# Transposes of x in four groups instead of three, the first two smaller, and meta rows loaded in two parts

## The chip, the cores and the metric

The kernel runs on one core of one Trainium2 chip. The metric is the device time of one execution in microseconds (us). The kernel before was timed in three runs.

## The reference, cut to what matters

One layer of a decoder trunk in float32. 16 meta tokens are put ahead of 256 tokens of x, which makes 272 tokens of 2048 features:

```python
h_res = concatenate([meta, x])                    # 272 x 2048
h = rmsnorm(h_res, pre_mix_g)
q_da, k_da, v_da, q_g, k_g, v_g, g_g, lr_g = split_cols(h @ w_in)   # 6144 + 16 columns
y = concatenate([diff_attention(...), gla(...)]) @ w_out            # 2048 x 2048
h_res = h_res + rmsnorm(y, post_mix_g)
y = conv_ffn(rmsnorm(h_res, pre_ffn_g), w_up, conv_w, conv_b, w_down)   # d_ff = 5632
out = (h_res + rmsnorm(y, post_ffn_g))[16:]
```

The change touches only the start: how x and the meta tokens reach the first columns of `h @ w_in`.

## The kernel before, in words

Every large product is done with split operands: a float32 matrix is written as hi + lo, both in a rounded format, and each product is hi·hi + hi·lo + lo·hi, three matmuls. Weights are streamed from memory by the queue of the sync engine SP in chunks of 128 x 1024 elements (512 KB) into eight buffers `raw`. A chunk has four blocks of 128 input features by 256 output columns. ScalarE (ACT) makes its hi part (`split_hi`, L358 to L362), then the lo part is made from both (`split_lo`, L364 to L367): by VectorE (DVE) for even chunks, by GpSimd (POOL) for odd ones (`lo_on_vector`, L50). TensorE (PE) then runs the chunk's 24 matmuls (`project_chunk`, L372 to L384), after waiting for the chunk's lo part. Four chunks make one pair of output tiles. Chunks 0 to 3 are the first pair; chunk c needs the input features 512·c to 512·c+511, that is tiles x_T 4c to 4c+3.

Those tiles come from x by transposes. SP loads x in four column blocks of 512 features (L451 to L454), each ahead of the weight chunk of the same number; the queue of ACT loads the first gain `pre_mix_g` (L555) and then the meta rows, 16 x 2048, in one transfer (L556). The step `x_T k` (L1335 to L1346) makes three transposes on PE into one of four side banks of PSUM: 16 meta rows and two blocks of 128 tokens. The step for k = 0 waits for the meta rows, each fourth for its block of x. ACT then writes `a_hi[k]`, scaled with the gain (L567). DVE writes a plain copy `xT[k]` (L864; for each fourth k ACT does it, L568) and `a_lo[k]` (L867), which frees the bank. For k < 8 a few matmuls without use follow (`busy`, L1317), five after k = 3 and one after each of the others.

All engines work their instructions in written order; nothing is planned at run time. `side_steps` (L55) says which small steps PE does after which chunk ("slot"). Before slot 0 stand the gain's transpose and x_T 0 to 7; after slot 0 x_T 8 to 11; after slot 1 x_T 12 to 15. On ACT the loop at L563 goes through the sixteen tiles and puts the first four hi splits among them:

```python
if k in (3, 5, 9, 11):
    split_hi(act_e, 0, (3, 5, 9, 11).index(k), first=True)
```

On DVE the loop at L859 does the lo split of chunk 0 after tile 3 and that of chunk 2 after tile 11; POOL does those of chunks 1 and 3 as soon as their hi parts are there (L508). PE waits before chunk c of the first pair for the release of its four tiles by DVE (L1530 to L1533). After the sixteen tiles ACT goes on with the hi split of chunk 4 and of later chunks, with the five squares of x (L577) between them.

Of the kernel before, what the change touches and what calls it, by code (L numbers as in the profile page):

```python
# [46 lines left out]
BANK = 512  # L47
# [7 lines left out]
def side_steps(slot, n_da, n_gla):  # L55


    steps = []
    if slot == -1:
        steps += [("pre_gain", 0)] + [("x_T", k) for k in range(8)]  # L60
    if slot in (0, 1):
        steps += [("x_T", k) for k in range(8 + 4 * slot, 12 + 4 * slot)]
    if slot == 5:
        steps += [("params", 0)]
    if slot == 6:
        steps += [("x_rms", 0)]
    if slot == 7:
        steps += [("lr", 0)]
    if slot == 8:
        steps += [("gates", hd) for hd in range(n_gla)]  # L70
    for h in range(n_da):
        for name, lag in (("scores", 0), ("probs_T", 3), ("attend", 5)):
            if slot == da_base(h) + lag:
                steps.append((name, h))
    for name, at in (("c_scores", C_BASE), ("c_T", C_BASE + 3), ("c_attend", C_BASE + 5)):
        if slot == at:
            steps.append((name, 0))
    if C_BASE + 8 <= slot < C_BASE + 8 + n_da:
        steps.append(("da_o_T", slot - C_BASE - 8))
    for hd in range(n_gla):  # L80
        for name, lag in (("v_T", 0), ("k_T", 3), ("kv", 5), ("gla_o", 7), ("gla_o_T", 10)):
            if slot == gla_base(hd) + lag:
                steps.append((name, hd))
    return steps
# [9 lines left out]
def da_base(h):  # L94


    return 12 * (h // 2 + 1) + 6 * (h % 2)


def gla_base(hd):  # L100
    return 60 + 8 * hd


def trunk(nc, x, meta_tokens, pre_mix_g, w_in, da_lambda, da_subln_g, gla_gate_w2, gla_gate_b, gla_norm_g,
          w_out, post_mix_g, pre_ffn_g, w_up, conv_w, conv_b, w_down, post_ffn_g, out):
    _, seq, d_model = x.shape
    n_meta = meta_tokens.shape[0]
    n_tok = n_meta + seq
# [55 lines left out]
    for slot in range(-1, IN1):  # L164
        for step in side_steps(slot, n_da, n_gla):
            first_turn[step] = turns
            turns += BANKS_OF[step[0]]
# [4 lines left out]
    with ExitStack() as ctx:  # L172
# [3 lines left out]
        def sem(name):  # L176
            return ctx.enter_context(nc.semaphore(name))
# [51 lines left out]
        def tile(t, n=1):  # L229
            return proj[:, t * n_tok:(t + n) * n_tok]  # L230
# [11 lines left out]
        def par_col(c):  # L242
            return par[:, c:c + 1]

        def tap(n, t):
# [4 lines left out]
        x_nat = tile(25, 23)[:, 0:3 * d_model].rearrange("p (t f) -> p t f", t=3)  # L250
# [51 lines left out]


        x_landed = [sem(f"x_landed{n}") for n in range(4)]
        meta_landed, gain_landed, par_landed, lam_landed, w2_landed, tail_landed, g_row_landed = (
            sem(n) for n in ("meta_landed", "gain_landed", "par_landed", "lam_landed", "w2_landed",
                             "tail_landed", "g_row_landed"))
        raw_landed = [sem(f"raw_landed{j}") for j in range(RAW)]
        hi_ready = sem("hi_ready")
# [48 lines left out]
        def split_hi(eng, rev, j, first=False):  # L358
            eng.wait_ge(raw_landed[j], rev * 16 + 16)
            if not first:  # L360
                eng.wait_ge(chunk_used, rev * RAW + (j - SPLIT + 1))
            eng.activation(w_hi[:, j % SPLIT, :], raw[:, j, :], ACT.Copy).then_inc(hi_ready, 1)  # L362
# [27 lines left out]
        def bank_of(step, n=0):  # L390
            return 4 + turn(step, n) % SIDE

        def await_free(pe, step, n=0):
            if turn(step, n) >= SIDE:
                pe.wait_ge(side_free[turn(step, n) % SIDE], turn(step, n) // SIDE)

        def await_full(eng, step, n=0):
            eng.wait_ge(side_full[turn(step, n) % SIDE], turn(step, n) // SIDE + 1)
# [5 lines left out]
        def full(step, n=0):  # L404
            return side_full[turn(step, n) % SIDE]
# [145 lines left out]
        def _(act_e):  # L551
            link = chain(act_e, act_chain)
            copy = lambda dst, src: act_e.activation(dst, src, ACT.Copy)

            act_e.dma_start(par_rows[0:KT, :], pre_mix_g[0].rearrange("(k p) -> k p", p=P)).then_inc(gain_landed, 16)  # L555
            act_e.dma_start(x_nat[0:n_meta, 2, :], meta_tokens).then_inc(meta_landed, 16)  # L556


            act_e.wait_ge(consts_made, 2)
# [3 lines left out]
            for k in range(KT):  # L563
                step = ("x_T", k)
                await_full(act_e, step)
                src = psum[:, bank_of(step), 0:n_tok]
                act_e.activation(a_hi[:, k, :], src, ACT.Copy, scale=par_col(G_PRE + k)).then_inc(x_hi_ready, 1)  # L567
                if k % 4 == 0:  # L568
                    copy(xT[:, k, :], src).then_inc(x_copied, 1)
                if k in (3, 5, 9, 11):  # L570
                    split_hi(act_e, 0, (3, 5, 9, 11).index(k), first=True)

            def x_square(n):

# [15 lines left out]
            for slot in range(IN1):  # L590
# [31 lines left out]
                for h in range(n_da):  # L622
# [9 lines left out]
                    if lag == 0:  # L632
# [7 lines left out]
                        for c in range(2):  # L640
                            for q, (_, _, a, b) in enumerate(DA_Q):
                                n = 2 * c + q
# [207 lines left out]
        def _(dve):  # L850
# [28 lines left out]
            for slot in range(IN1):  # L879
# [45 lines left out]
                if slot == 6 or slot % 4 == 3 and slot > 3:  # L925

                    p = slot // 4 if slot % 4 == 3 else 0
                    _, t0, kind = pairs[p]
                    a = Q0 if kind == "q" else 0
                    dve.wait_ge(chunk_used, 4 * p + 4)  # L930
                    for m in range(2):
                        dve.tensor_tensor(tile(t0 + m)[:, a:n_tok], psum[:, 2 * (p % 2) + m, 0:n_tok - a],  # L932
                                          rb[:, a:n_tok], ALU.mult).then_inc(tiles_evacuated, 1)
# [14 lines left out]
                for h in range(n_da):  # L948
                    lag = slot - da_base(h)
                    if lag == 0:  # L950

                        step = ("scores", h)
                        for c in range(2):
                            await_full(dve, step, 1 + c)
                            for q, (_, _, a, b) in enumerate(DA_Q):
                                n = 2 * c + q
                                ins = dve.tensor_reduce(s_max[:, n:n + 1], psum[:, bank_of(step, 1 + c), a:b], AX.X,
                                                        ALU.max)
                        link(ins)
                        dve.tensor_scalar(s_bias[:], s_max[:], -da_scale, None, ALU.mult).then_inc(bias_ready, 1)  # L960
# [343 lines left out]
        def _(pe):  # L1304
            def transposes(bank, sources):

                for col, src in sources:
                    rows, cols = src.shape
                    mm = pe.transpose(psum[0:cols, bank, col:col + rows], src, ident[0:rows, 0:rows])  # L1309
                return mm  # L1310
# [6 lines left out]
            def busy(bank, n):  # L1317

                for _ in range(n):
                    pe.matmul(psum[:, bank, 0:P], ones[:], ident[:], start=True, stop=True)  # L1320
# [14 lines left out]
            def x_T(step):  # L1335
                k = step[1]
                if k == 0:
                    pe.wait_ge(meta_landed, 16)
                if k % 4 == 0:
                    pe.wait_ge(x_landed[k // 4], 16)  # L1340
                await_free(pe, step)
                f = slice(k * P, (k + 1) * P)
                transposes(bank_of(step), [(0, x_nat[0:n_meta, 2, f]), (n_meta, x_nat[:, 0, f]),
                                           (n_meta + P, x_nat[:, 1, f])]).then_inc(full(step), 1)
                if k < 8:
                    busy(3, 5 if k == 3 else 1)  # L1346

            def x_rms(step):

# [162 lines left out]
            def gla_o_T(step):  # L1512
                hd = step[1]
                pe.wait_ge(og_scaled, 2 * hd + 2)
                for v in range(2):
# [3 lines left out]
                        .then_inc(full(step, v), 1)  # L1519

            emit = {"pre_gain": pre_gain, "params": params, "x_T": x_T, "x_rms": x_rms, "lr": lr, "gates": gates,
                    "scores": scores, "probs_T": probs_T, "attend": attend, "c_scores": c_scores, "c_T": c_T,
                    "c_attend": c_attend,
                    "da_o_T": da_o_T, "v_T": v_T, "k_T": k_T, "kv": kv, "gla_o": gla_o, "gla_o_T": gla_o_T}

            for step in side_steps(-1, n_da, n_gla):
                emit[step[0]](step)
            for slot in range(IN1):
                p, kind = slot // 4, pairs[slot // 4][2]
                if p == 0:  # L1530

                    for k in range(4 * slot, 4 * slot + 4):
                        await_evacuated(pe, ("x_T", k))  # L1533
                if slot % 4 == 0 and p >= 2:
                    pe.wait_ge(tiles_evacuated, 2 * (p - 1))
                project_chunk(pe, slot // RAW, slot % RAW, 2 * (p % 2), Q0 if kind == "q" else 0, n_tok)
                for step in side_steps(slot, n_da, n_gla):
                    emit[step[0]](step)
# [93 lines left out]
            for bank in range(8):  # L1632
                t, h, n = bank // 4, bank // 2 % 2, bank % 2
# [31 lines left out]
```

## Time and profile before

| what | value |
|---|---|
| median of 3 runs (lowest to highest) | 1294.6 us (1293.31 to 1294.68) |
| span of the profiled execution | 1294.8 us |
| PE busy | 1272.3 us, 98% |
| DVE, ACT, POOL busy | 664.1, 609.6, 505.7 us |
| memory traffic | 209.30 MB read, 163 GB/s over the span |

The profiled execution is given by its span alone; it lies 0.2 us above the median and 0.1 us above the slowest of the three runs. The page divides the span into 40 slices; the change lies in the first two of them, so windows of the trace are more use here than the page.

### The profile page before, as it was taken

The numbers are of one execution on the slowest core, as the hardware profiler recorded it, in microseconds if no ns is written. First come the engines' busy times: TensorE is split into PE (matmuls) and PEld (weight loads), VectorE is DVE, ScalarE is ACT, GpSimd is POOL, SyncE is SP. The second block draws the span as 40 slices with busy tenths as digits, with TensorE's granted clock in tenths as the row PEclk, the third lists the DMA queues.
The fourth block names the chain that finished last, engine by engine and source line by source line (L and its number), as shares of the span: only waits on it lengthen the run. The fifth ranks groups of instructions, "written<-read, shape, count | busy, mean of one in ns | idle before, by whom it ended". The sixth has DMA issues, their size and how long they took to land.

```text
span 1294.8 us, 24260 instructions
## 1 busy us (share of the span) xinstructions
PE 1272.3 (98%) x9194; PEld 1193.0 (92%) x9194; DVE 664.1 (51%) x963; ACT 609.6 (47%) x928; POOL 505.7 (39%) x231
## 2 busy tenths in 40 slices
PE   8989999999999999899999999999999999999997
PEld 7989999998888999899999999999999988888885
DVE  5353433447455534876666666666666652222224
ACT  5543443444555544554444545445454454444444
POOL 2232232232233443433444444444444444444443
PEclk8989999999999999899999999999999999999999
DMA  9534444443344556255565555656556555555551
GB/s 267 160 98 133 129 137 135 120 148 114 116 133 151 184 174 201 85 161 178 169 188 182 183 179 170 193 179 181 178 175 194 178 195 190 186 187 185 191 178 65
DMA packets 178105, 212.08 MB, mean 164 GB/s; under 512 B 8659, under 2 KB 164842, under 8 KB 177914
## 3 DMA queue, kind: packets, MB, share of 16 engines
q1 hardware_dynamic: 177850, 210.24, 52.2%
q10 hardware_dynamic: 208, 1.19, 0.3%
q8 instruction: 33, 0.54, 0.2%
q14 instruction: 14, 0.11, 0.0%
HBM read 209.30 MB, written 2.10 MB: 163 GB/s over the span
## 4 chain that ended last, share of the span: by engine, by line
PE 93%; DVE 5%; ACT 1%; DMA 1%; issue 0%; DVEq 0%; ACTq 0%
PE psum L382 66%; PE psum L1611 18%; PE psum L1309 2%; PE psum L1393 1%; DVE a_lo L1146 1%; DVE a_lo L876 1%; PE psum L1420 1%; DVE temp L946 1%; PE psum L1488 1%; PE psum L1395 1%; DMA proj<-in_meta_tokens 1%; PE psum L1421 1%; DVE w_lo L366 1%; PE psum L1639 0%; PE psum L1365 0%
## 5 line engine op out<-in xcount | busy, mean ns | idle before, releaser
L366 POOL TENSOR_TENSOR w_lo<-raw,w_hi 128x1024 fp32r<-128x1024 f32 x196 | 485.9, 2479 | 760.9 <-ACT w_hi L362 760.9
L382 PE MATMUL psum<-a_hi,w_hi 128*128 128x258 f32 (+1 forms) x2432 | 700.7, 288 | 3.5 <-DVE w_lo L366 1.4
L382 PE MATMUL psum<-a_hi,w_lo 128*128 128x258 f32 (+1 forms) x2432 | 697.6, 287 | 0.0
L382 PE MATMUL psum<-a_lo,w_hi 128*128 128x258 f32 (+1 forms) x2432 | 694.7, 286 | 0.0
L362 ACT ACTIVATE w_hi<-raw 128x1024 fp32r<-128x1024 f32 x392 | 412.4, 1059 | 526.2 <-PE psum L382 396.8
L366 DVE TENSOR_TENSOR w_lo<-raw,w_hi 128x1024 fp32r<-128x1024 f32 x196 | 261.6, 1335 | 447.5 <-ACT w_hi L362 446.5
L382 PEld LDWEIGHTS psum<-a_hi,w_hi 128*128 128x128 f32 x2432 | 465.2, 191 | 10.8 <-issue 7.0
L382 PEld LDWEIGHTS psum<-a_hi,w_lo 128*128 128x128 f32 x2432 | 465.2, 191 | 0.0
L382 PEld LDWEIGHTS psum<-a_lo,w_hi 128*128 128x128 f32 x2432 | 464.1, 191 | 0.0
L1611 PE MATMUL psum<-w_hi,a_hi 128*128 128x512 f32 x336 | 132.1, 393 | 0.0
L1611 PE MATMUL psum<-w_lo,a_hi 128*128 128x512 f32 x336 | 132.0, 393 | 0.0
L1611 PE MATMUL psum<-w_hi,a_lo 128*128 128x512 f32 x336 | 131.8, 392 | 0.0
L1201 DVE SCALAR_TENSOR_TENSOR proj<-proj,par 128x256 f32<-128x256 f32 x88 | 111.4, 1265 | 38.5 <-ACT proj L772 38.5
L1611 PEld LDWEIGHTS psum<-w_lo,a_hi 128*128 128x128 f32 x336 | 63.1, 188 | 14.4
L1611 PEld LDWEIGHTS psum<-w_hi,a_lo 128*128 128x128 f32 x336 | 63.1, 188 | 14.3
L1611 PEld LDWEIGHTS psum<-w_hi,a_hi 128*128 128x128 f32 x336 | 63.2, 188 | 14.1
L1204 DVE SCALAR_TENSOR_TENSOR proj<-proj,par 128x256 f32<-128x256 f32 x88 | 42.7, 485 | 11.6 <-DVE proj L1201 2.6
L772 ACT ACTIVATE proj<-proj,par 128x256 f32<-128x256 f32 x88 | 47.6, 589 | 1.6 <-DVE proj L1195 1.5
L778 ACT ACTIVATE proj<-proj 128x256 f32<-128x256 f32 x44 | 18.4, 420 | 63.0 <-DVE proj L1204 63.0
L1195 DVE TENSOR_TENSOR proj<-psum,rb 128x258 f32<-128x258 f32 x88 | 33.4, 421 | 15.5 <-PE psum L382 13.5
L1309 PE MATMUL psum<-ident,proj 128*128 128x128 f32 (+5 forms) x130 | 22.9, 277 | 5.6 <-DVE proj L932 3.7
L932 DVE TENSOR_TENSOR proj<-psum,rb 128x272 f32<-128x272 f32 (+1 forms) x48 | 18.6, 428 | 17.6 <-PE psum L382 17.5
(230 smaller groups left out, 673.6 us busy)
## 6 DMA issues: line engine op xcount, KB each, us to landing
raw<-in_w_up SPq DMA_DIRECT2D x176, 512.0 KB, 3.6
raw<-in_w_in SPq DMA_DIRECT2D x96, 512.0 KB, 3.8
raw<-in_w_down SPq DMA_DIRECT2D x88, 512.0 KB, 3.6
raw<-in_w_out SPq DMA_DIRECT2D x32, 512.0 KB, 3.5
proj<-in_x SPq DMA_DIRECT2D x4, 512.0 KB, 9.3
temp<-in_post_ffn_g ACTq DMA_DIRECT2D x1, 1024.0 KB, 8.0
out<-proj SPq DMA_DIRECT2D x2, 512.0 KB, 2.6
out<-proj SPq DMA_DIRECT2D x4, 256.0 KB, 2.6
```

The costliest lines, as they stand in the source:

```text
L362: eng.activation(w_hi[:, j % SPLIT, :], raw[:, j, :], ACT.Copy).then_inc(hi_ready, 1)
L366: eng.tensor_tensor(w_lo[:, j % SPLIT, :], raw[:, j, :], w_hi[:, j % SPLIT, :], ALU.subtract)\
L382: mm = pe.matmul(psum[:, bank + m, 0:t1 - t0], w[:, j % SPLIT, cols], a[:, k, t0:t1], start=(k == 0 and step == 0), stop=(k == KT - 1 and ...
L772: act_e.activation(c_sb[:, t, :], u_sb[:, m, NM:NQ], ACT.Identity, scale=tap(2, i * 2 + (m + NF * half)), bias=tap(3, i * 2 + (m + NF * ha ...
L778: act_e.activation(c_sb[:, m, :], c_sb[:, m, :], ACT.Silu).then_inc(silu_done, 1)
L876: dve.tensor_tensor(a_lo[:, k, 0:NQ], heads_tile(k), a_hi[:, k, 0:NQ], ALU.subtract)\
L932: dve.tensor_tensor(tile(t0 + m)[:, a:n_tok], psum[:, 2 * (p % 2) + m, 0:n_tok - a], rb[:, a:n_tok], ALU.mult).then_inc(tiles_evacuated, 1)
L1195: dve.tensor_tensor(u_sb[:, m, :], psum[:, t, 0:NQ], rb2[:], ALU.mult).then_inc(tiles_evacuated, 1)
L1201: dve.scalar_tensor_tensor(out=c_sb[:, t, :], in0=u_sb[:, m, 1:1 + seq], scalar=tap(1, w), in1=c_sb[:, t, :], op0=ALU.mult, op1=ALU.add).t ...
L1204: dve.scalar_tensor_tensor(out=c_sb[:, t, :], in0=u_sb[:, m, 0:seq], scalar=tap(0, w), in1=c_sb[:, t, :], op0=ALU.mult, op1=ALU.add).then_ ...
L1309: mm = pe.transpose(psum[0:cols, bank, col:col + rows], src, ident[0:rows, 0:rows])
L1611: mm = pe.matmul(psum[:, bank, :], a[:, j // 2, t * P:(t + 1) * P], w[:, j % SPLIT, n * BANK:(n + 1) * BANK], start=(first and s == 0), st ...
```

## The change

The diff, whole but for the list of semaphores:

```diff
@@ side_steps @@
     if slot == -1:
-        steps += [("pre_gain", 0)] + [("x_T", k) for k in range(8)]
-    if slot in (0, 1):
-        steps += [("x_T", k) for k in range(8 + 4 * slot, 12 + 4 * slot)]
+        steps += [("pre_gain", 0)] + [("x_T", k) for k in range(4)]
+    if slot in (0, 1, 2):
+        steps += [("x_T", k) for k in range(4 + 4 * slot, 8 + 4 * slot)]
@@ ScalarE @@
+            act_e.dma_start(x_nat[0:n_meta, 2, 0:BANK], meta_tokens[:, 0:BANK]).then_inc(meta_landed, 16)
             act_e.dma_start(par_rows[0:KT, :], pre_mix_g[0].rearrange("(k p) -> k p", p=P)).then_inc(gain_landed, 16)
-            act_e.dma_start(x_nat[0:n_meta, 2, :], meta_tokens).then_inc(meta_landed, 16)
+            act_e.dma_start(x_nat[0:n_meta, 2, BANK:d_model], meta_tokens[:, BANK:d_model]).then_inc(meta_rest_landed, 16)
@@
-                if k in (3, 5, 9, 11):
-                    split_hi(act_e, 0, (3, 5, 9, 11).index(k), first=True)
+                if k % 4 == 3:
+                    split_hi(act_e, 0, k // 4, first=True)
@@ TensorE, x_T @@
                 if k == 0:
                     pe.wait_ge(meta_landed, 16)
+                if k == 4:
+                    pe.wait_ge(meta_rest_landed, 16)
                 if k % 4 == 0:
                     pe.wait_ge(x_landed[k // 4], 16)
...
-                if k < 8:
-                    busy(3, 5 if k == 3 else 1)
+                if k < 4:
+                    busy(3, 8 if k == 3 else 1)
```

PE now does x_T 0 to 3, chunk 0, x_T 4 to 7, chunk 1, x_T 8 to 11, chunk 2, x_T 12 to 15, chunk 3. ACT makes the hi part of chunk c after `a_hi` of tile 4c+3. The meta rows come as a block of 512 features ahead of the gain on ACT's queue and the other 1536 behind it. Eight useless matmuls follow x_T 3, one each x_T 0 to 2, none x_T 4 to 7. Everything else is as before.

## Rows read from the trace of the kernel before

**Rows 1.** The page: busy time of the engines, and the chain that ended last.

```profile
PE 1272.3 (98%) x9194; PEld 1193.0 (92%) x9194; DVE 664.1 (51%) x963; ACT 609.6 (47%) x928; POOL 505.7 (39%) x231
...
PE 93%; DVE 5%; ACT 1%; DMA 1%; issue 0%; DVEq 0%; ACTq 0%
```

**Rows 2.** Chain of waits from 0 to 80 us: start, us, what.

```profile
1.32 6.70 DMA proj<-in_meta_tokens
...
17.93 2.87 PE psum L382 x24
...
25.48 3.22 DVE w_lo L366
28.70 0.14 issue
28.84 13.50 PE psum L382 x96
...
56.03 3.02 PE psum L382 x24
```

**Rows 3.** DMA issues that touch 0 to 1 us, with time to landing.

```profile
proj<-in_x SPq DMA_DIRECT2D x1, 512.0 KB, 5.8
proj<-in_pre_mix_g ACTq DMA_DIRECT2D x1, 8.0 KB, 3.7
```

**Rows 4.** Timeline to chunk 0: start, us, engine, line, operation, [idle before <-releaser].

```profile
0.83 0.44 SPq L453 DMA_DIRECT2D proj<-in_x  x1
...
8.06 0.60 PE L1309 MATMUL psum<-ident,proj 16*128 16x16 f32 x3 [1.88 <-DMA proj<-in_meta_tokens]
...
13.82 1.23 DVE L366 TENSOR_TENSOR w_lo<-raw,w_hi 128x1024 fp32r<-128x1024 f32 x1
...
16.62 1.05 ACT L362 ACTIVATE w_hi<-raw 128x1024 fp32r<-128x1024 f32 x1
...
17.68 0.36 PE L382 MATMUL psum<-a_hi,w_hi 128*128 128x258 f32 x1
17.75 2.41 POOL L366 TENSOR_TENSOR w_lo<-raw,w_hi 128x1024 fp32r<-128x1024 f32 x1 [13.10 <-ACT w_hi L362]
```

**Rows 5.** Timeline, transposes x_T 8 to 11 and chunk 1.

```profile
20.73 2.19 PE L1309 MATMUL psum<-ident,proj 16*128 16x16 f32 x12
...
22.24 0.50 DVE L867 SCALAR_TENSOR_TENSOR a_lo<-psum,par,a_hi 128x272 fp32r<-128x272 f32 x1 [2.56 <-ACT xT L553]
...
22.68 0.36 PE L382 MATMUL psum<-a_hi,w_hi 128*128 128x258 f32 x1
```

**Rows 6.** Timeline, transposes x_T 12 to 15 and the work behind them.

```profile
25.40 3.29 DVE L366 TENSOR_TENSOR w_lo<-raw,w_hi 128x1024 fp32r<-128x1024 f32 x1
25.74 2.19 PE L1309 MATMUL psum<-ident,proj 16*128 16x16 f32 x12
...
28.35 1.05 ACT L362 ACTIVATE w_hi<-raw 128x1024 fp32r<-128x1024 f32 x1
29.02 0.43 DVE L864 COPY xT<-psum 128x272 f32<-128x272 f32 x1
...
29.78 0.43 DVE L864 COPY xT<-psum 128x272 f32<-128x272 f32 x1
```

**Rows 7.** Windows: stretch, length, busy PE, PEld, DVE, ACT, POOL, PEclk (1.00 full), DMA share, GB/s.

```profile
7.00:8.00 1.00, 0.00 (x0) 0.00 (x0) 0.00 (x0) 0.00 (x0) 0.00 (x0) 1.00 1.06 291
8.00:9.00 1.00, 0.94 (x6) 0.71 (x6) 0.00 (x0) 0.22 (x1) 0.00 (x0) 0.83 1.04 373
...
25.73:28.84 3.11, 2.20 (x14) 1.37 (x13) 3.11 (x2) 2.42 (x6) 1.88 (x1) 1.00 1.09 368
28.84:33.10 4.26, 4.26 (x23) 4.26 (x24) 3.67 (x8) 4.26 (x7) 0.60 (x1) 0.60 1.06 340
...
78.00:83.00 5.00, 5.00 (x20) 4.02 (x21) 0.82 (x3) 1.54 (x3) 0.00 (x0) 0.50 0.88 298
```

**Rows 8.** Waits of SP's queue, 0 to 80 us: who waited for whom, total, times, longest.

```profile
SPq L356 <- POOL w_lo L366: 24.6, 5, 8.6
```

More of the change, by code:

```diff
@@ L304, in trunk @@
         x_landed = [sem(f"x_landed{n}") for n in range(4)]
-        meta_landed, gain_landed, par_landed, lam_landed, w2_landed, tail_landed, g_row_landed = (
-            sem(n) for n in ("meta_landed", "gain_landed", "par_landed", "lam_landed", "w2_landed",
+        meta_landed, meta_rest_landed, gain_landed, par_landed, lam_landed, w2_landed, tail_landed, g_row_landed = (
+            sem(n) for n in ("meta_landed", "meta_rest_landed", "gain_landed", "par_landed", "lam_landed", "w2_landed",
                              "tail_landed", "g_row_landed"))
```

## The prediction

> **What bounds the kernel now.** I read the page first. PE is busy 98% of the span, and 93% of the chain that ended last runs over it [rows 1]. So the rest of the kernel has next to nothing that could swallow a delay of PE or hand one back; what counts is at which moment PE leaves the stretch that the change touches. The second view is the chain of waits over the first 80 us [rows 2]. It enters through the landing of the meta rows, runs over PE to the end of chunk 1, leaves PE once for DVE's lo split of chunk 2, and then stays on PE for 96 matmuls (chunks 2 to 5) from 28.84 to 42.34 us. A chunk later on takes 3.02 us, chunk 1 took 25.73 - 22.68 = 3.05. With the last two of the four at 3.02, chunk 3 ended at 42.34 - 6.04 = 36.3 us. That is my yardstick: what the change does to 36.3 it does to the end. SP's queue waits for the splits there, not the splits for SP [rows 8], so loads don't bound this stretch.
>
> **The third view, the timeline, gives the pace of one group of four tiles.** Call T the start of its first transpose on PE.
> PE: the twelve transposes take 2.19 us [rows 5, 6].
> ACT: in the last group, T = 25.74, the hi split behind the fourth `a_hi` runs from 28.35 to 29.40, so it begins at T+2.6 and ends at T+3.7 [rows 6].
> DVE: the first `a_lo` starts at 22.24, with T = 20.73, and takes 0.50, so it ends at T+2.0 [rows 5]. Each further tile takes 0.76 us, the step between two copies (29.02 and 29.78) [rows 6]. Four tiles are through at T+4.3.
> Lo split: on DVE it comes behind this and takes 1.23 us [rows 4], so it ends at T+5.5. On POOL it begins 0.08 us after the hi split and takes 2.41 [rows 4], which gives T+6.15, with PE's reaction T+6.2.
>
> **Part 1: the groups come one later, and their hi splits with them.** This is the costly part. Before, PE ran x_T 4 to 7 ahead of chunk 0, and the hi split of chunk 1 stood after tile 5; it was done at 17.67, and POOL's lo split ran under chunk 0 (17.75 to 20.16) [rows 4]. Likewise x_T 8 to 11 ran ahead of chunk 1 and served chunk 2. Each split chain thus had a whole chunk of 3 us of PE work over it, and still chunk 2 was late: PE finished its transposes at 27.93 and started at 28.84, when DVE's split ended [rows 2, 6]. That split took 3.29 us instead of 1.23 because POOL's split of chunk 3 ran beside it; I take it that this stall goes, since in the new order POOL has nothing to do while chunk 2 is split.
> Now PE ends chunk c, does the four transposes that chunk c+1 needs, and has nothing behind them: the next instruction in its queue is chunk c+1 itself. From T to its start:
> - chunk 1 (POOL): 6.2 us, of which 2.2 are transposes, 4.0 idle
> - chunk 2 (DVE): 5.5 us, 3.3 idle
> - chunk 3 (POOL): 6.2 us, 4.0 idle
>
> Together 17.9 us, 11.3 of them idle. Behind the waiting PE stands everything; ACT, DVE and POOL have no work that could be drawn forward, as their queues wait for the same tiles. Below this I see no cheaper bound than the hi split moved by a few tenths. Above, transposes at half clock would make each group about 1.4 longer (below).
>
> **Part 2: the start.** PE waited 1.88 us for the meta rows, until 8.05 [rows 4]; they landed at 1.32 + 6.70 = 8.02 [rows 2]. x block 0, issued at 0.83, landed 5.8 later, at 6.6 [rows 3, 4]. The first quarter of the meta rows is now issued first on ACT's queue. The trace has no transfer of its size: 8 KB took 3.7 us and the whole 128 KB 6.7. From 0.82 on that means a landing between 4.5 and 7.5; I take one before 6.6, so x block 0 releases the first transpose at 6.65, a gain of 1.4. The gain's transfer, now 0.5 us later, lands near 5.0 and its transpose is done before that. The other meta rows, issued about 1 us after the first, have until after chunk 0.
> From T = 6.65 the pace above gives lo split 0 on DVE done at 6.65 + 4.3 + 1.23 = 12.2 us, where chunk 0 starts, since PE's transposes and eight useless matmuls are through by about 10.5. If the clock is at half, as before in this place, the pace is that of before, 15.05 - 8.06 = 7.0 [rows 4], and the start is 13.65. Chunk 0 started at 17.68, because x_T 4 to 7 stood ahead of it. So the start gives 4.0 to 5.5 us. One useless matmul fewer is nothing beside this.
>
> **Part 3: the clock.** Before chunk 2 PE idled 0.9 us, and right after it the granted clock was at its lower level: 0.60 on average over 28.84 to 33.10, where 23 matmuls took the 4.26 us [rows 7]. Chunks 2 to 5 took 13.50 us against 4 x 3.04 = 12.16, so one fall cost 1.34 us. It also fell after the idle stretch before 8.05. The new order has four idle stretches, 1.7 us ahead of chunk 0 and three of 3.3 to 4.0. I charge each chunk one fall: 4 x 1.34 = 5.4. The lower end is 0, were the clock never to fall; the upper is below.
> The row shows the clock at full through x_T 12 to 15 and the idle time behind them (PEclk 1.00, PE busy 2.20 of 3.11 us), and down right after [rows 7]. The Trainium skill ("TensorE: Matmul & The Clock Gate", Part 4) says that transposes don't count as PE-busy in the way matmuls do. By that rule the useless matmuls left out behind x_T 4 to 7 are missed, and the clock may stay down through the groups too; that is rival B.
>
> **Sum.** 12.2 + 4 x 3.04 + 17.9 + 5.4 = 47.7 us for the end of chunk 3, against 36.3: +11.4.
>
> **What comes behind.** ACT has five squares to do between its next hi splits (now some 2 us later against chunk 3's end), but chunk 4's hi split stands ahead of them, and by the same durations each later chunk is split 1 us or more ahead of PE. I take nothing, with 0.5 us as the upper bound for the row of the rms. The weight stream has eight buffers and is released by the same splits, so it shifts with PE.
>
> The profiled execution has a span of 1294.8 us, 0.2 above the median of the runs. 1294.8 + 11.4 = 1306.2; brought to the median, 1306.0 us.
>
> **Rivals.**
> A. The chain is as forecast but the clock never falls: without the 5.4, +6.0, 1300.6 us. For it: single falls before followed on quiet stretches of different kinds. Against: 0.9 us of idle was already enough behind the same transposes. Chance 0.12.
> B. The clock stays down over the whole stretch. For it: from 78 to 83 us, after an idle stretch of 3.7 us, PE was busy throughout with 20 small operations and the clock stood at 0.50 [rows 7]. The price: one fall cost 1.34 us in about 3.4 us at the lower level (0.60 over 4.26), 0.39 per us. A chunk of 3.04 then takes 5.0, four of them +7.8, and the three groups of 2.2 take 3.6, +4.2, together 12.0 instead of 5.4: 1312.6 us. Against: chunks are dense, and the clock came back within chunk 2 before. Chance 0.08.
> C. The other side: the waits between the groups are hidden, so that PE runs 4 x 3.04 + 3 x 2.2 = 18.8 us from 12.2 on and ends chunk 3 at 31.0, 5.3 earlier: 1289.3 us. It is one mechanism, the time from the last transpose of a group to its chunk, and it decides at 5.3 / 3 = 1.8 us per group. It would need the split chain to start before its fourth tile. The rows say 3.3 to 4.0, and ACT's order in the diff puts the hi split behind tile 4c+3. Chance 0.04.
> D. The meta part doesn't land sooner than the whole did (three transfers share the engines from 1.3 us on): the first transpose stays at 8.05, chunk 0 starts at 15.05, +2.9 on the forecast: 1308.9 us. This is the case in which the change doesn't do what it says. Chance 0.12.
> The forecast itself has the rest, 0.64, with its own range from 1303 to 1309.5 (start 12.2 or 13.65, one fall more or less of 1.34, the 0.5 behind).
>
> **How the numbers follow.** A, the forecast, D and half of B lie between 1300 and 1311.5; that holds well over 8 in 10, and I pull the ends in no further, since A and B are the bounds of the one unknown price. What this kernel's measurement can tell from no change is 0.2%, 2.6 us. Slower by more: everything but C and a remainder of mixtures, 0.95. Within 0.2%: 0.02. Faster: 0.03.
>
> **What would show it.** In the profile after: the first transpose near 6.7 us with x as its releaser; chunk 0 at 12 to 14; PE idle 3 to 4 us ahead of each of chunks 1, 2 and 3, released by a lo split, POOL's, DVE's, POOL's; DVE's split of chunk 2 at 1.2 us instead of 3.29; the granted clock below 1.00 in each of the four chunks; chunk 3 ending near 48 us; and from there on the same distances as before. I am wrong if PE finds chunk 1 split within 1.8 us of its last transpose, or if a wait far behind takes up the delay.

## The result: 1.1% slower, and the profile after

The changed kernel takes 1307.3 us (median of 4 runs, 1306.04 to 1309.2) against 1294.0 (median of 4, 1293.31 to 1294.68): +13.3 us, ratio 1.011 with an interval from 1.0085 to 1.0136. Forecast were 1306.0 us and a range from 1300 to 1311.5. The profiled execution has a span of 1306.8 us, 12.0 more than [rows 1]'s.

The page after: busy time, and the chain that ended last. PE's busy time grew by 1.6 us, its idle time from 1294.8 - 1272.3 = 22.5 to 1306.8 - 1273.9 = 32.9 us: 10.4 of the 12.0 us are idle time.

```profile
PE 1273.9 (97%) x9192; PEld 1193.9 (91%) x9192; DVE 664.8 (51%) x963; ACT 609.0 (47%) x928; POOL 505.7 (39%) x231
...
PE 93%; DVE 5%; ACT 1%; issue 1%; DMA 0%; POOL 0%; DVEq 0%; ACTq 0%
```

The chain of waits after (start, us, what), to be read against [rows 2]. It enters through the gain and no longer through the meta rows, and leaves PE ahead of each of the four chunks, where before it left PE ahead of chunk 2 alone:

```profile
1.31 4.83 DMA proj<-in_pre_mix_g
...
8.48 0.83 PE psum L1310 x3
...
14.60 1.24 DVE w_lo L366
15.83 0.14 issue
15.96 3.12 PE psum L382 x24
19.08 2.14 PE psum L1310 x12
...
22.76 2.35 POOL w_lo L366
25.11 0.14 issue
25.25 4.46 PE psum L382 x24
...
33.92 1.14 DVE w_lo L366
35.06 0.14 issue
35.20 4.57 PE psum L382 x24
39.77 2.13 PE psum L1310 x12
...
43.44 2.37 POOL w_lo L366
45.80 0.14 issue
45.94 10.39 PE psum L382 x72
...
70.01 3.02 PE psum L382 x24
```

PE's waits over the whole execution after: who waited for whom, total, times, longest. Before, the waits for a lo split came to 1.4 us in two; now there are 8.1 for POOL's and 4.1 for DVE's. All later waits (3.7, 3.2 us and so on) are as before.

```profile
PE psum L382 <- POOL w_lo L366: 8.1, 2, 4.0
PE psum L382 <- DVE w_lo L366: 4.1, 3, 3.4
PE psum L1310 <- DVE proj L933: 3.7, 1, 3.7
```

Windows after over chunks 1, 2 and 3 (columns as in [rows 7]): each chunk runs partly at the lower clock, as chunk 2 did before.

```profile
25.25:29.71 4.46, 4.46 (x25) 4.32 (x25) 0.00 (x0) 0.00 (x0) 0.00 (x0) 0.66 1.10 346
35.20:39.77 4.57, 4.57 (x25) 4.44 (x25) 0.00 (x0) 0.00 (x0) 0.00 (x0) 0.64 0.38 115
45.94:50.27 4.33, 4.33 (x25) 4.33 (x26) 0.93 (x1) 4.33 (x9) 2.39 (x1) 0.68 0.76 238
```

Chunks 3 to 5 end at 45.94 + 10.39 = 56.33, so chunk 3 ended near 50.3, against 36.3 before: 14.0 us late. The last chunk of this stretch, at 56.03 before [rows 2], begins at 70.01: still 14.0. The span shows 12.0. Of the 2.0 between them, about 1.5 are one fall of the clock that the traced execution of before had and that of after had not. The rows are the window right behind the small matmuls of one attention head, first before, then after:

```profile
203.00:207.00 4.00, 4.00 (x21) 3.93 (x20) 0.83 (x3) 1.77 (x8) 0.00 (x0) 0.57 0.44 131
```

```profile
217.00:221.00 4.00, 4.00 (x34) 4.00 (x33) 1.56 (x6) 2.84 (x9) 0.00 (x0) 1.00 0.40 125
```

The 72 matmuls there took 10.73 us before and 9.24 after. The remaining 0.5 us was not traced further. So single executions of one kernel differ by where the clock falls; those of before in the comparisons below (17, 23 and 29 executions) ran from 1288.7 to 1296.5 us, with medians of 1293.4 to 1293.6. That is why the experiments are judged by medians and intervals first, and a profile only for what happened within it.

### The profile page after: what moved, and what is told of

It is laid out like the page before. It is cut to its first block, busy times and chain, and to the rows that moved or that the text cites. A ratio compares the mean times of both kernels' runs of the same rounds, so it can differ in the third digit from the quotient of the medians.

```text
span 1306.8 us, 24257 instructions
## 1 busy us (share of the span) xinstructions
PE 1273.9 (97%) x9192; PEld 1193.9 (91%) x9192; DVE 664.8 (51%) x963; ACT 609.0 (47%) x928; POOL 505.7 (39%) x231
## 3 DMA queue, kind: packets, MB, share of 16 engines
q10 hardware_dynamic: 240, 1.19, 0.2%
## 4 chain that ended last, share of the span: by engine, by line
PE 93%; DVE 5%; ACT 1%; issue 1%; DMA 0%; POOL 0%; DVEq 0%; ACTq 0%
PE psum L382 66%; PE psum L1614 18%; PE psum L1310 2%; PE psum L1396 1%; DVE a_lo L1147 1%; DVE a_lo L877 1%; PE psum L1423 1%; DVE temp L947 1%; PE psum L1491 1%; PE psum L1398 1%; PE psum L1424 1%; PE psum L1642 0%; PE psum L1368 0%; DVE w_lo L366 0%; DVE proj L1159 0%
```

## The experiments

All ratios are against the kernel before on the same chips. The changed kernel has 1.011 (1.0085 to 1.0136).

**e1, the groups alone** (meta rows whole, behind the gain, as before):

```diff
-            act_e.dma_start(x_nat[0:n_meta, 2, 0:BANK], meta_tokens[:, 0:BANK]).then_inc(meta_landed, 16)
             act_e.dma_start(par_rows[0:KT, :], ...).then_inc(gain_landed, 16)
-            act_e.dma_start(x_nat[0:n_meta, 2, BANK:d_model], ...).then_inc(meta_rest_landed, 16)
+            act_e.dma_start(x_nat[0:n_meta, 2, :], meta_tokens).then_inc(meta_landed, 16)
```

> The changed kernel with the meta rows loaded whole and behind the gain, as before; only the four groups and the split order are new. Theory (serial split chain plus clock falls is the whole loss, the split meta load brings nothing because the gain, now second, lands at 6.14 us): chunk 0 starts at 15 to 16 us, PE idles 3.3 to 4.0 us ahead of chunks 1, 2 and 3, and the time is within 1.5 us of the changed kernel, 1306 to 1309 us. Rival (the split meta load is worth the 1.4 us that the forecast gave it, or costs by contention): 1308.5 or more if it helped, under 1305.5 if it hurt.

Measured: 1307.6 us, ratio 1.0112 (1.009 to 1.0135). The groups are the whole loss, together with what this run changes beside them: ACT's order of the hi splits (taken alone in e6) and the useless matmuls, none behind x_T 4 to 7 and eight instead of five behind x_T 3. The split load neither helps nor hurts the changed kernel beyond what can be told. Chunk 0 started at 15.36.

**e2, the meta load alone** (the kernel before, with the quarter ahead of the gain):

```diff
+            act_e.dma_start(x_nat[0:n_meta, 2, 0:BANK], meta_tokens[:, 0:BANK]).then_inc(meta_landed, 16)
             act_e.dma_start(par_rows[0:KT, :], ...).then_inc(gain_landed, 16)
-            act_e.dma_start(x_nat[0:n_meta, 2, :], meta_tokens).then_inc(meta_landed, 16)
+            act_e.dma_start(x_nat[0:n_meta, 2, BANK:d_model], ...).then_inc(meta_rest_landed, 16)
```

> The kernel before with the meta load in two parts, the quarter ahead of the gain, nothing else. Theory (the gain became the transfer that PE waits for): gain's transpose near 6.2 us, first transpose of x near 8.0 to 8.4, time within 1 us of before. Forecast's step, as rival: first transpose of x near 6.7 us and the time 1.4 us or more below before.

Measured: 1294.76 us, ratio 1.0017 (1.0006 to 1.0029). Not 1.4 us faster, but 1.4 us slower by the medians and 0.8 to 3.7 by the interval, which is more than the 1 us that I had allowed; why it is slower and not the same was not found. The gain's transpose waited until 6.26, and the first of x ran at 7.51. (The trace of this kernel caught a good execution, span 1288.3: its transposes up to 14 us ran at the short durations, 0.53 us for three, where before they took 0.83. The median is the measure.)

**e3, the changed kernel with the gain first**:

```diff
+            act_e.dma_start(par_rows[0:KT, :], ...).then_inc(gain_landed, 16)
             act_e.dma_start(x_nat[0:n_meta, 2, 0:BANK], meta_tokens[:, 0:BANK]).then_inc(meta_landed, 16)
-            act_e.dma_start(par_rows[0:KT, :], ...).then_inc(gain_landed, 16)
```

> The changed kernel with the gain first on ACT's queue, then the meta quarter, then the rest. Theory: gain lands near 4.6 us and the first transpose of x moves from 8.4 to about 6 to 7 us; chunk 0 starts 1.5 to 3.5 us earlier (12.2 to 14.5 instead of 15.96); the time is 1.5 to 3.5 us below the changed kernel, unless a clock fall ahead of chunk 0 takes 1.3 of it back. Rival (the landing order doesn't matter, PE's slow clock sets the start): chunk 0 within 0.5 us of 15.96, no change.

Measured: 1305.69 us, 1.6 below the changed kernel by the medians, ratio 1.0102 (1.0079 to 1.0125), so the intervals of the two overlap. The trace says what happened. Loads that touch the first microseconds, first after, then e3 (size, us to landing): whichever of the two small transfers stands second takes 4.8 or 4.9 us instead of 3.1.

```profile
proj<-in_meta_tokens ACTq DMA_DIRECT2D x1, 32.0 KB, 3.1
proj<-in_pre_mix_g ACTq DMA_DIRECT2D x1, 8.0 KB, 4.8
```

```profile
proj<-in_meta_tokens ACTq DMA_DIRECT2D x1, 32.0 KB, 4.9
proj<-in_pre_mix_g ACTq DMA_DIRECT2D x1, 8.0 KB, 3.1
```

The timeline of PE at the start, first after, then e3. In the changed kernel PE waits for the gain, then does eight useless matmul passes behind its transpose, and only then the first transposes of x, at 8.41. With the gain first they start at 6.61:

```profile
6.19 0.28 PE L1310 MATMUL psum<-ident,proj 16*128 16x16 f32 x1 [1.50 <-DMA proj<-in_pre_mix_g]
6.40 2.08 PE L1321 MATMUL psum<-ident,ones 128*128 128x128 f32 x8
8.41 0.90 PE L1310 MATMUL psum<-ident,proj 16*128 16x16 f32 x3
```

```profile
4.83 1.85 PE L1321 MATMUL psum<-ident,ones 128*128 128x128 f32 x8
6.61 0.60 PE L1310 MATMUL psum<-ident,proj 16*128 16x16 f32 x3
```

Chunk 0 started at 12.35 in e3, 3.6 us earlier than after. But chunks 1 and 2 then took 5.41 and 5.12 us, with the clock at 0.52 and 0.56, where after they took 4.46 and 4.57: nearly half of what the start had given went back.

Of those 3.6 us only a part is the gain's place. The trace of e3 caught the transposes ahead of chunk 0 at their short duration, 0.53 us for three, that of after at the long one, 0.83. The trace of e4, the next run, has the loads in the order of after and the short duration, and its chunk 0 starts at 13.16:

```profile
13.16 0.36 PE L382 MATMUL psum<-a_hi,w_hi 128*128 128x258 f32 x1 [1.09 <-DVE w_lo L366]
```

So 15.96 - 13.16 = 2.8 us are the pace, and 13.16 - 12.35 = 0.8 the gain's place. At the long duration the gain's place gives 15.96 - 14.47 = 1.5 (chunk 0 of e12, below, against after). That is in line with the 1.6 by the medians.

**e4, all hi splits behind tile 3**:

```diff
-                if k % 4 == 3:
-                    split_hi(act_e, 0, k // 4, first=True)
+                if k == 3:
+                    for c in range(4):
+                        split_hi(act_e, 0, c, first=True)
...
-                if k % 4 == 3 and lo_on_vector(k // 4):
-                    split_lo(dve, 0, k // 4)
+                if k in (3, 7):
+                    split_lo(dve, 0, (k - 3) // 2)
```

> The changed kernel with all four first hi splits behind tile 3 on ACT (they need no tile of x, only the weights), and DVE's lo split of chunk 2 behind tile 7. Theory (the hi and lo splits behind each group make the wait): from the first transpose of a group to its chunk 4.4 us instead of 6.2, 5.5, 6.2, so idle about 2.2 each, 4.7 us less in all; released by DVE's a_lo, not by a lo split; time near 1302.6 us, lower by up to 3 more if clock falls go too. Rival (the waits come from the evacuation of the tiles or the landing of data anyway): under 1.5 us gained.

Measured: 1307.44 us, ratio 1.0116 (1.0096 to 1.0137): nothing gained. The last two groups took 4.5 and 4.6 us to their chunks, as expected, the first 5.9. The cause of that stands in ACT's timeline: the hi split of chunk 3 waited for its weights, and `a_hi` of tile 4, transposed near 16.7, stood behind it. And chunks 3 to 5 took 11.81 us, where after they took 10.39.

```profile
17.33 1.06 ACT L362 ACTIVATE w_hi<-raw 128x1024 fp32r<-128x1024 f32 x1 [2.03 <-DMA raw<-in_w_in]
...
18.29 0.47 ACT L568 ACTIVATE a_hi<-psum,par 128x272 fp32r<-128x272 f32 x1
```

**e10, the same with the split of chunk 3 behind tile 7**:

```diff
+                if k == 3:
+                    for c in range(3):
+                        split_hi(act_e, 0, c, first=True)
+                if k == 7:
+                    split_hi(act_e, 0, 3, first=True)
```

> e4 with the hi split of chunk 3 moved behind tile 7. Theory (in e4 ACT stood before a_hi of tile 4 for the weights of chunk 3, which landed at 17.3 us): the first group too takes 4.4 to 4.6 us from its first transpose to its chunk, as the two others did; chunk 3 ends about 1.5 to 2 us earlier than in e4 and 6 earlier than in the changed kernel; time 3 to 6 us below the changed kernel. Rival (what is gained on the splits is lost to more low clock): again no gain over the changed kernel, within 1.5 us.

Measured: 1308.27 us, ratio 1.0106 (1.0082 to 1.013). Again nothing, and the rival was right. In the chain of waits the groups are as short as they were meant to be: 19.23 to 23.70, 29.19 to 33.86 and 39.36 to 44.06, that is 4.5, 4.7 and 4.7 us instead of 6.2, 5.5 and 6.2, the evacuation by DVE (its copies and `a_lo`) as the last link. But each chunk now ran wholly at the lower clock. Windows of e10 over chunks 1, 2 and 3:

```profile
23.70:29.19 5.49, 5.49 (x25) 5.26 (x25) 2.63 (x1) 0.00 (x0) 1.55 (x1) 0.50 1.10 353
33.86:39.36 5.50, 5.50 (x25) 5.27 (x25) 0.00 (x0) 0.00 (x0) 0.00 (x0) 0.50 0.00 0
44.06:49.50 5.44, 5.43 (x25) 5.44 (x26) 1.12 (x2) 5.44 (x11) 2.38 (x1) 0.50 0.32 96
```

Idle time saved: 17.9 - 13.9 = 4.0 us in three groups. Paid for it: 3 x 5.48 - (4.46 + 4.57 + 4.33) = 3.1 us, and another 0.4 in chunk 4, which took 3.36 us instead of 3.01. At chunk 6 the traced execution is 0.4 us ahead of that of after (56.35 against 56.76), at its end 1.7 behind: between 120 and 130 us its window shows a granted clock of 0.83, where that of after shows 1.00.

**e5, useless matmuls in the idle time**:

```diff
                 if k < 4:
                     busy(3, 8 if k == 3 else 1)
+                elif k % 4 == 3:
+                    busy(3, 14)
```

> The changed kernel with 14 useless matmuls more on PE behind tiles 7, 11 and 15, where it idled 3.3 to 4.0 us. Theory (each idle stretch costs its own length and one fall of the clock worth 1.34 us): the chunks start when they did, but take 3.05 instead of 4.3 to 4.5 us; time 4 us below the changed kernel, near 1303. Rival (the idle time alone is the cost, or the useless matmuls delay the chunks as much as they give): within 1 us of the changed kernel.

Measured: 1303.7 us, 3.6 below the changed kernel, ratio 1.0079 (1.0055 to 1.0103). The groups took 6.2, 5.5 and 6.2 us as in the changed kernel; the clock didn't fall. Windows of e5 over chunks 1 and 2:

```profile
25.39:28.51 3.12, 3.12 (x25) 2.98 (x25) 0.00 (x0) 0.00 (x0) 0.00 (x0) 1.00 1.06 341
34.00:37.12 3.12, 3.12 (x25) 2.98 (x25) 0.00 (x0) 0.00 (x0) 0.00 (x0) 1.00 0.57 173
```

So of the 13.3 us, 3.6 are the clock in these chunks and 13.3 - 3.6 = 9.7 the idle time and the later groups themselves.

**e12, all mends on the changed kernel** (e10's splits, e3's order of loads, `busy(3, 8)` behind tiles 7, 11 and 15).

> The changed kernel with all three mends: hi splits early as in e10, gain first, eight useless matmuls behind tiles 7, 11 and 15. Theory (each cost is separate and adds): chunk 0 at 12.4, three groups of 4.4 us to their chunks, no fall of the clock, chunk 3 ending at 12.4 + 12.2 + 13.3 = 37.9 us against 36.3 in the traced execution of before: 0 to 2 us above before, 1294 to 1296, some 12 below the changed kernel. Rival (one PE order is worse than the other by more than the pieces say): 1299 or more.

Measured: 1296.88 us, ratio 1.0022 (1.0011 to 1.0034): 10.4 below the changed kernel, 3 above before. That is 0.9 above the range that I had expected. The traced execution has groups of 4.47 us and chunks of 3.11, as expected, but chunk 0 at 14.47 and not at 12.4: the three transposes of a tile took 0.83 us there, and the sixteen passes that the useless matmuls behind x_T 3 make took 3.20. e10's splits, worth nothing alone, count once the clock holds: e10 and e3 alone brought -1.0 and +1.6 us, e5 3.6, together 4.2, and all three at once 10.4.

**e7, PE's new order with ACT's old one**:

```diff
-                if k % 4 == 3:
-                    split_hi(act_e, 0, k // 4, first=True)
+                if k in (3, 5, 9, 11):
+                    split_hi(act_e, 0, (3, 5, 9, 11).index(k), first=True)
```

> The changed kernel with ACT's old order of the hi splits (behind tiles 3, 5, 9, 11). Theory: with PE's new order the transposes and their evacuation are uncovered whatever ACT does: about 5.4, 5.5 and 4.4 us from a group's first transpose to its chunk, 2.6 us less than 17.9 in all; time 2.6 us below the changed kernel, near 1304.7, that is some 10.5 above before. Rival (ACT's order is the larger half): under 1300.

Measured: 1311.95 us, ratio 1.0145 (1.0118 to 1.0171): 4.6 above the changed kernel, where I had expected 2.6 below. The timeline of e7 around the group of tiles 8 to 11 shows what I had left out. The hi splits of chunks 2 and 3 are both done when DVE comes to its lo split of chunk 2, and POOL has begun its own 0.16 us ahead; DVE's takes 3.27 us instead of 1.2, and chunk 2 starts 8.1 us after the group's first transpose, where I had expected 5.5. The chunks behind it were slower too: chunk 2 took 5.48 us (after: 4.57) and chunks 3 to 5 11.61 (after: 10.39). The stall and these chunks make 2.6 + 0.9 + 1.2 = 4.7 of the 7.2 us between expectation and result. The traced execution also had a granted clock of 0.83 from 170 to 180 us, where that of after had 1.00.

```profile
28.04 2.19 PE L1310 MATMUL psum<-ident,proj 16*128 16x16 f32 x12
...
32.55 2.34 POOL L366 TENSOR_TENSOR w_lo<-raw,w_hi 128x1024 fp32r<-128x1024 f32 x1 [9.21 <-ACT w_hi L362]
32.71 3.27 DVE L366 TENSOR_TENSOR w_lo<-raw,w_hi 128x1024 fp32r<-128x1024 f32 x1
36.12 0.55 PE L382 MATMUL psum<-a_hi,w_hi 128*128 128x258 f32 x1 [5.89 <-DVE w_lo L366]
```

**e6, ACT's new order in the kernel before** (the reverse edit of e7, on the kernel before).

> The kernel before with only ACT's order of the first hi splits changed (behind tiles 3, 7, 11, 15 instead of 3, 5, 9, 11). Theory (the loss needs PE's new order, in which no chunk covers a split): chunk 3's split comes later, so POOL no longer blocks DVE's split of chunk 2, which takes 1.2 instead of 3.3 us; chunk 3 may wait up to 0.5; time between 2.5 us below before and 0.5 above. Rival (the late hi splits alone make the loss): 5 us or more above before.

Measured: 1293.54 us, ratio 1.0002 (0.9988 to 1.0017): no difference. With x_T one group ahead of the chunks, the late hi splits cost nothing. In its timeline DVE's split of chunk 2 takes 1.21 us, and PE waits 1.19 us for POOL's split of chunk 3 instead:

```profile
23.28 1.21 DVE L366 TENSOR_TENSOR w_lo<-raw,w_hi 128x1024 fp32r<-128x1024 f32 x1
...
27.83 2.38 POOL L366 TENSOR_TENSOR w_lo<-raw,w_hi 128x1024 fp32r<-128x1024 f32 x1 [7.85 <-ACT w_hi L362]
...
30.36 0.35 PE L382 MATMUL psum<-a_hi,w_hi 128*128 128x258 f32 x1 [1.19 <-POOL w_lo L366]
```

**e8, the kernel before with early splits**:

```diff
-                if k in (3, 5, 9, 11):
-                    split_hi(act_e, 0, (3, 5, 9, 11).index(k), first=True)
+                if k in (3, 5):
+                    split_hi(act_e, 0, (k - 3) // 2, first=True)
+                if k == 7:
+                    for c in (2, 3):
+                        split_hi(act_e, 0, c, first=True)
...
-                if k % 4 == 3 and lo_on_vector(k // 4):
-                    split_lo(dve, 0, k // 4)
+                if k in (3, 7):
+                    split_lo(dve, 0, (k - 3) // 2)
```

> The kernel before with the first hi splits behind tiles 3, 5, 7, 7 and DVE's lo split of chunk 2 behind tile 7. Theory (PE's 0.9 us wait ahead of chunk 2 came from POOL's split beside DVE's): the wait goes, 0.9 us, and the fall of the clock behind it, 1.34, if the clock doesn't fall for the transposes alone; time 0.9 to 2.3 us below before. Rival (the time is set elsewhere, or the earlier hi splits delay the tiles ahead of chunk 0): no gain or slower by up to 1 us.

Measured: 1291.29 us, ratio 0.9985 (0.9971 to 0.9999), 2.2 us below before. PE has no wait left ahead of chunks 1 to 3, and the granted clock stays at 1.00 over all three: behind the twelve transposes alone, 2.12 us, it didn't fall; behind the same transposes and 0.9 us of idle time it did, in before, e2 and e11.

**e11, the kernel before with the gain first and the meta load in two parts** (e2's edit, the gain ahead of both).

> The kernel before with the meta load in two parts but the gain ahead of both. Theory (e2 gave nothing since the gain had become the last to land): the first transpose of x at 6.5 to 6.8 us instead of 7.9, chunk 0 about 1 us earlier, time 1 to 1.5 us below before and 1.5 to 3 below e2. Rival (PE's x block 1, landing near 10 us, takes the gain back): within 0.5 us of before.

Measured: 1290.55 us, ratio 0.9975 (0.9961 to 0.9988), 3 us below before and 4.2 below e2. The first transpose of x ran at 6.83. The gain is larger than the 1 to 1.5 us expected, and the trace can't say where the rest comes from: it caught the slowest of the twelve executions (1295.44 us, chunk 0 at 16.73, against 17.68 in that of before).

**e9, both**:

> The kernel before with the early splits of e8 and ACT's queue in the order gain, meta quarter, meta rest. Theory: e8's gain over before stays, about 2 us, and the first transpose of x comes 1 to 2 us earlier (6.0 to 6.7 instead of 7.9 us), so chunk 0 starts 1 to 1.5 us earlier: near 1290 us, 3 to 4 below before. Rival (the start is bound by the transposes' own pace and the clock, whatever lands first): no more than e8, 1291 to 1292.

Measured: 1289.37 us, ratio 0.9965 (0.9951 to 0.9979): 4.2 us below before and the lowest median of all (the interval overlaps those of e8 and e11). Until chunk 8 PE has one wait, for the constants at the very start.

## Why the prediction was right, point by point

- **The bound and the yardstick.** Right. 14.0 us late at chunk 3's end, and 14.0 still when the last chunk of the first 80 us starts. No later wait took anything up; what differs by the end, 2.0 us, is mostly the clock elsewhere.
- **The pace of a group and the three waits.** Right to a tenth. From a group's first transpose to its chunk the chain shows 25.25 - 19.08 = 6.17, 35.20 - 29.71 = 5.49 and 45.94 - 39.77 = 6.17 us, forecast 6.2, 5.5, 6.2; the releasers are POOL, DVE, POOL. e6 and e7 show that it is PE's order that matters. The lesson of the stall was right for the changed kernel (DVE's split took 1.21 us) and forgotten for e7.
- **The start.** This step failed. The sum had chunk 0 at 12.2; it started at 15.96, 3.8 us later. Two terms were wrong. The first is the step "the gain lands near 5.0 and its transpose is done before that": it landed at 1.31 + 4.83 = 6.14, and eight passes of useless matmuls stood between it and x, so that the first transpose of x ran at 8.41 and not at 6.65. Taking the gain's own row, 3.7 us from first place [rows 3], for a transfer in second place was the error. (The meta quarter landed at 0.82 + 3.1 = 3.9, sooner than the 4.5 to 7.5 forecast, and x block 0 at 0.83 + 4.9 = 5.7; PE waited for neither.) The second is the pace: the sum has 5.5 us from the first transpose to chunk 0, and they were 7.5, near the 7.0 that the prediction gives for the clock at half and left out of its sum. PE's useless matmuls were through at 15.66 instead of 10.5. The traces of e3 and e4 part the two: about 2.8 of the 3.8 us are the pace, about 1.0 the gain and the passes behind it.
- **The clock.** Charged with four falls of 1.34, 5.4 us. Three chunks had one, worth 1.42 + 1.53 + 1.29 = 4.2 over chunks of 3.04; chunk 0 took 3.12 us. Term by term: -1.2 us. The fourth charge stood in the wrong place: the slow pace lay in the transposes ahead of chunk 0, and there it cost 2.8. The price of one fall was right here only: e10 shows 2.4 us per chunk after idle stretches that were shorter.
- **The sum.** 47.7 + 3.8 - 1.2 = 50.3. The two errors went against each other, so that the time came out 1.3 us from the forecast for a stretch that was 2.6 off; that is luck. Without the later lucky 1.5 the difference of the spans would have been above 13, as that of the medians is.
- **The profiled time against the median.** I set the span of 1294.8 beside the median of 1294.6 as if they were the same measure. The profiled execution after was 1308.55 us for a span of 1306.8, 1.75 us more. By that, the execution of [rows 1] was one of some 1296.5, 2.5 above its median of 1294.0, where that of after was 1.25 above its own. That accounts for 13.3 by the medians against 12.0 by the spans. It did not touch the forecast, which is the median plus 11.4.
- **The rivals.** C (the waits are hidden) was excluded by the waits themselves. A (the chain as forecast, the clock never down) came about only with e5's useless matmuls. B (the clock down over the whole stretch) did not occur in the changed kernel: its groups' transposes ran at their short durations, 2.19 us for twelve in all three, as before [rows 5, 6]. Half of it occurred in e10, where the chunks ran wholly at the lower clock (5.5 us, B had priced 5.0) and the groups mostly did not. D's premise was wrong, though its result was nearly right: chunk 0 at 15.96 instead of 15.05, for the gain and the pace instead of the meta rows.

Why e10 falls deeper than the changed kernel with less idle time was not settled: the clock was at 0.50 for the whole of each chunk, but no run varied the length of the idle time alone. Its length is not the whole of it: e3 has the splits of the changed kernel and the same idle stretches, 4.0 and 3.4 us, only some 3 us sooner, and its chunks 1 and 2 took 5.41 and 5.12 us. So that e10's shorter waits brought on the deeper falls is not shown.

## What to carry to other kernels

An engine that fills its waits with its own preparing work needs that work one stage ahead: here transposes for chunk c+1 directly before chunk c+1 cost 3.3 to 4.0 us each time, because four hands (PE, ACT, DVE, POOL) had to pass them on while PE had nothing else. When a load is moved to the front of a queue, look at what it was moved ahead of: the 8 KB gain, not the 128 KB, became the one that PE waited for. And cost an idle stretch on PE with the clock behind it: shorter waits gained nothing (e10) until useless matmuls kept the clock up (e12).

## What the runs showed of the hardware that I had not expected

- Two small transfers on one queue, at the start beside the loads of x and weights: the first landed 3.1 to 3.4 us after its issue (2.9 in e11), the second 4.8 to 5.2 us after its own, whichever of them was the 8 KB and whichever the 32 KB one. With the 128 KB one behind it, the 8 KB one took 3.0 to 3.7.
- 24 matmuls of chunk 1 took 3.12 us with the clock at 1.00 (e5), 4.46 at 0.66 (after) and 5.49 at 0.50 (e10).
- In the first 14 us of the changed kernel the windows show a PEclk of 1.00 (first row below), yet three transposes took 0.83 us there, as they did before where the windows show 0.50 (second row), and 0.53 later. The durations are what to go by in that stretch.

```profile
8.00:15.00 7.00, 7.00 (x33) 5.96 (x32) 3.46 (x8) 3.18 (x6) 0.00 (x0) 1.00 1.07 351
```

```profile
10.00:11.00 1.00, 1.00 (x6) 0.81 (x5) 0.84 (x3) 0.32 (x1) 0.00 (x0) 0.50 1.10 367
```

- One and the same start runs at either pace: of the kernels whose loads are as before, e8 had chunk 0 at 16.08 us where the traced execution of before had it at 17.68 [rows 4]; with the changed loads, e4 had it at 13.16 and the changed kernel at 15.96. What sets the pace of an execution was not found.
- An idle stretch is not always followed by a fall: in e6 PE waited 1.19 us behind the matmuls of chunk 2, and the windows from 28 to 36 us show 1.00 throughout.
